# Transposes of two convolution branches and of four head pairs' outputs, moved from TensorE to VectorE blocks and GpSimd's transfers

## What is computed

```python
def reference(x, mem, ...):
    for i in range(DEPTH):                     # DEPTH = 2
        h = _rms_norm(x, pre_norm[i])
        proj = h @ w_in[i]
        tok, q_mem, gate = ...                 # 3*1536 | 512 | 2048 columns
        if i % 2 == 0:
            tok_out = _short_conv_mixer(tok, conv_w[i // 2])      # gate_b * conv3(gate_c * x_in)
        else:
            tok_out = _diff_attention_mixer(tok, positions, ...)  # (softmax1 - lam*softmax2) @ v, normalised per head
        mem_n = _rms_norm(mem, mem_norm[i])
        cross_out = _memory_cross_attention(q_mem, mem_n, w_kv_mem[i])
        y = concatenate([tok_out, cross_out]) * silu(gate) @ w_out[i]
        x = x + _rms_norm(y, post_norm[i])
```

## Time and profile before

| what | value |
|---|---|
| median of three runs | 946.15 us (945.61 to 946.81) |
| the profiled execution, its own time | 946.67 us |
| its span, first to last instruction | 944.9 us |
| granted TensorE clock, mean | 0.998 |
| busy: TensorE, VectorE, ScalarE, GpSimd | 933.8, 636.3, 503.6, 17.2 us |
| share of the chain that ended last: TensorE, VectorE, ScalarE, DMA | 88%, 5%, 2%, 2% |

### The profile page before, as it was taken

One profiled execution on the slowest core, in us unless ns is written; L12 is line 12 of the kernel. 1 busy time (PEld: TensorE's weight loads), 2 busy tenths in 40 slices (PEclk: granted clock), 3 DMA queues, 4 the chain that ended last, 5 costly groups with the idle time before them and its releaser, 6 DMA issues.

```text
span 944.9 us, 12669 instructions
## 1 busy us (share of the span) xinstructions
PE 933.8 (99%) x4752; PEld 789.4 (84%) x4752; DVE 636.3 (67%) x834; ACT 503.6 (53%) x801; POOL 17.2 (2%) x41
## 2 busy tenths in 40 slices
PE   9999999999999999999999999999999999999996
PEld 7888888888888888888888888888888888888885
DVE  5878766754565475555595558557787888888555
ACT  6867553344344443444465555447586576675542
POOL 0000200000000000000000003000000000000000
PEclk9999999999999999999999999999999999999999
DMA  9757585766766666676566658565755746745652
GB/s 330 244 164 230 170 258 177 213 198 214 221 188 191 187 193 220 228 240 231 178 234 192 184 151 255 171 208 154 216 176 159 222 146 187 221 145 173 222 197 89
DMA packets 124894, 188.45 MB, mean 199 GB/s; under 512 B 7277, under 2 KB 66989, under 8 KB 124330
## 3 DMA queue, kind: packets, MB, share of 16 engines
q1 hardware_dynamic: 122138, 178.80, 60.9%
q10 hardware_dynamic: 1680, 6.85, 2.1%
q0 software_dynamic: 1024, 2.10, 0.9%
HBM read 178.82 MB, written 2.10 MB: 191 GB/s over the span
## 4 chain that ended last, share of the span: by engine, by line
PE 88%; DVE 5%; ACT 2%; DMA 2%; issue 2%; SPq 0%; DVEq 0%; POOL 0%; ACTq 0%; POOLq 0%
PE psum L480 19%; PE psum L481 19%; PE psum L482 19%; PE psum L419 17%; PE psum L420 9%; DVE lo_ring L1037 2%; DMA stage_area<-in_mem_dram 1%; PE psum L499 1%; ACT hi_ring L720 1%; DMA layer_area<-layer_area 1%; ACT layer_area L1001 1%; PE psum L661 1%; DMA raw_ring<-in_w_in_dram 0%; ACT stage_area L810 0%; DVE layer_area L1463 0%
## 5 line engine op out<-in xcount | busy, mean ns | idle before, releaser
L1037 DVE TENSOR_TENSOR lo_ring<-raw_ring,hi_ring 128x1024 fp32r<-128x1024 f32 x318 | 385.6, 1222 | 249.0 <-ACT hi_ring L720 248.4
L720 ACT ACTIVATE hi_ring<-raw_ring 128x1024 fp32r<-128x1024 f32 x318 | 335.4, 1061 | 363.0 <-PE psum L482 253.0
L419 PE MATMUL psum<-hT_split,hi_ring 128*128 128x512 f32 x832 | 292.9, 397 | 0.4 <-DVE lo_ring L1037 0.4
L420 PE MATMUL psum<-hT_split,lo_ring 128*128 128x256 f32 x832 | 232.1, 279 | 0.0
L419 PEld LDWEIGHTS psum<-hT_split,hi_ring 128*128 128x128 f32 x832 | 156.1, 188 | 38.8 <-issue 2.0
L480 PE MATMUL psum<-hi_ring,hT_split 128*128 128x512 f32 x480 | 187.0, 390 | 0.4 <-DVE lo_ring L1037 0.4
L481 PE MATMUL psum<-lo_ring,hT_split 128*128 128x512 f32 x480 | 186.8, 389 | 0.0
L482 PE MATMUL psum<-hi_ring,hT_split 128*128 128x512 f32 x480 | 186.8, 389 | 0.0
L420 PEld LDWEIGHTS psum<-hT_split,lo_ring 128*128 128x128 f32 x832 | 156.8, 188 | 0.1
L480 PEld LDWEIGHTS psum<-hi_ring,hT_split 128*128 128x128 f32 x480 | 90.1, 188 | 19.3 <-issue 0.7
L482 PEld LDWEIGHTS psum<-hi_ring,hT_split 128*128 128x128 f32 x480 | 90.1, 188 | 18.9
(11 more groups left out here) (227 smaller groups left out, 754.4 us busy)
## 6 DMA issues: line engine op xcount, KB each, us to landing
raw_ring<-in_w_in_dram SPq DMA_DIRECT2D x224, 512.0 KB, 3.9
raw_ring<-in_w_out_dram SPq DMA_DIRECT2D x64, 512.0 KB, 4.1
raw_ring<-in_w_kv_mem_dram SPq DMA_DIRECT2D x30, 512.0 KB, 4.3
layer_area<-layer_area SPq DMA_DIRECT2D x48, 64.0 KB, 3.7
x_residual<-in_conv_w_dram ACTq DMA_DIRECT2D x3, 768.0 KB, 6.4
stage_area<-in_mem_dram SPq DMA_DIRECT2D x8, 256.0 KB, 6.6
x_residual<-in_x_dram SPq DMA_DIRECT2D x2, 1024.0 KB, 8.6
layer_area<-in_post_norm_dram ACTq DMA_DIRECT2D x2, 1024.0 KB, 6.2
```

What stands on the lines that cost most here:

```text
L419: mm(o, hi[:, k, P * c:P * (c + 1)], X[:, kt, :], start=kt == 0, stop=False)
L420: last = mm(o[:, SEQ:], lo[:, k, P * c:P * (c + 1)], X[:, kt, 0:SEQ], start=False, stop=kt == KT - 1)
L720: run(whi[:, slot, :], raw[:, slot, :], ACT.Copy).then_inc(hi_ready, 1)
L1037: V_.tensor_tensor(wlo[:, slot, :], raw[:, slot, :], whi[:, slot, :].bitcast(f32), SUB)\
```

## The change

Branches 0 and 1 of the convolution, and the outputs of head pairs 0 to 3, are now turned as the memory probabilities were: VectorE turns 32x32 blocks, GpSimd issues 16 transfers, and the result is read from SBUF. Branch 2 and pairs 4 and 5 stay with TensorE. The block turn of layer 0's memory probabilities moves from the last gate group to the first row group of mix 0.

```diff
@@ GpSimd
+        cross_move(0)
+        for j in range(MIXES - 1):
+            pool.wait_ge(b_blocks_turned, 2 * (j + 1))
+            for a, b in QUADRANTS:
+                nc.gpsimd.dma_start(S[32 * b:32 * b + 32, 3072 + 256 * a:3072 + 256 * (a + 1)],
+                                    b_blocks[32 * a:32 * a + 32, 256 * b:256 * (b + 1)]).then_inc(b_blocks_moved, 16)
+        cross_move(1)
+        for p in range(PAIRS - 2):
+            pool.wait_ge(o_blocks_turned, p + 1)
+            for a, b in QUADRANTS:
+                nc.gpsimd.dma_start(oT[32 * b:32 * b + 32, a], o_blocks[32 * a:32 * a + 32, b]).then_inc(o_blocks_moved, 16)
@@ TensorE
-                at = {3: lambda: branch_turn(j - 1)} if j and g == 0 else {4: first_cross_values} if (j, g) == (0, 1) else {}
+                at = {4: first_cross_values} if (j, g) == (0, 1) else {}
...
-            if not first and not second:
-                in_keys[3] = lambda: diff_out_turn(p - 2, p * 8)
@@ ScalarE
+        def branch_rows_high(j):
+            act.wait_ge(b_blocks_moved, 256 * (j + 1))
+            for t in range(TT):
+                last = run(branch_view(j, 0, t), bT[:, t], ACT.Copy)
+            last.then_inc(b_hi, 1)
@@ VectorE
-                     at={2: lambda: cross_blocks(0), 3: lambda: cross_vm_low(0)})
+                     at={3: lambda: cross_vm_low(0)})
...
-            row_group(u, at={5: lambda: branch_low(j - 1)} if j else {})
+            row_group(u, at={1: lambda: branch_blocks(j - 1)} if j else {1: lambda: cross_blocks(0)})
+
+            row_group(u + A_UNITS, at={2: lambda: branch_rows_low(j - 1)} if j else {2: lambda: cross_weights_low(0),
+                                                                                      6: first_cross_branch})
...
+        def out_blocks(p):
+            dve.wait_ge(on_ready, p + 1)
+            V_.transpose(o_blocks.rearrange("p b r g -> p g b r"), o_sb.rearrange("p g (b r) -> p g b r", b=4))\
+              .then_inc(o_blocks_turned, 1)
+
+        def out_moved(st, p, parity):
+            dve.wait_ge(o_blocks_moved, p * 256 + 256)
+            rows_, gate = (v.rearrange("p c (t q) -> p (c t) q", t=TT) for v in (br1, sgate[parity]))
+            V_.scalar_tensor_tensor(rows_, oT.rearrange("p a r g -> p g (a r)"), subg, gate, MULT, MULT).then_inc(o_taken, 1)
+            dve.wait_ge(o_taken, p + 2)
+            split_branch(st, br1, bass.ds(p * 2, 2), in_order=True)
...
+            def norm_and_turn():
+                out_norm(st, p - 2, parity)
+                out_blocks(p - 2)
...
-                in_query[3] = lambda: out_norm(st, p - 2, parity)
-                in_gate[1] = lambda: out_take(st, p - 2, parity)
+                in_query[3] = norm_and_turn
             column_group(G + 2, c + 2, u + 2 * B_UNITS, s, val1, at=in_gate)
+            if not first and not second:
+                out_moved(st, p - 2, parity)
             dve.wait_ge(bank_free, G + 3)
             st.did(silu_twice(p + (MIXES + 3), tanh1, val1, sgate[parity]))
```

More of the change, by code:

```diff
@@ L158, in build @@
     o_sb = l1(5376).rearrange("p (g e) -> p g e", g=4)
+    vm_flat = vm.rearrange("p m e -> p (m e)")
+    o_blocks = vm_flat[:, 0:512].rearrange("p (b r g) -> p b r g", b=4, g=4)
+    oT = vm_flat[:, 512:1024].rearrange("p (a r g) -> p a r g", a=4, g=4)
     o_sq = l1(5888).rearrange("p (g e) -> p g e", g=4)
@@ L175, in build, with branch_view @@
     u_rows, u_before, u_part, b_rows = (rows(S[:, 1024 * i:1024 * (i + 1)]) for i in range(4))
+    b_blocks = S[:, 2048:3072]
+    bT = S[:, 3072:4096].rearrange("p (a c t r) -> p t c a r", a=4, c=4, t=TT)
+    def branch_view(j, first, t):
+        return XC[:, 4 * j:4 * j + 4, first + P * t:first + P * (t + 1)].rearrange("p c (a r) -> p c a r", a=4)
     xg_flat = xgate.rearrange("p h t -> p (h t)")
@@ L243, in build @@
     u_shifted, taps_loaded = sem("u_shifted"), [sem(f"conv_taps_loaded{j}") for j in range(MIXES)]
+    b_blocks_turned, b_blocks_moved = sem("branch_blocks_turned"), sem("branch_blocks_moved")
+    o_blocks_turned, o_blocks_moved = sem("o_blocks_turned"), sem("o_blocks_moved")
     b_ready, b_turned, b_hi = sem("branch_rows_ready"), sem("branch_rows_turned"), sem("branch_hi")
@@ L385, in _, with cross_move @@
                                 pattern=[[-1, P]], channel_multiplier=1).then_inc(const_ready, 1)
-        for l in range(DEPTH):
+        def cross_move(l):
             pool.wait_ge(xblocks_turned, 4 * (l + 1))
@@ L633, in _, with diff_values @@
                 cross_values(1)
-        def diff_values(p):
+        def diff_values(p, first=False):
             pe.wait_ge(wt_ready, p * 16 + 16)
+            if not first:
+                pe.wait_ge(o_blocks_turned, p)
             for h in range(2):
@@ L643, in diff_values, with diff_out_turn @@
             last.then_inc(pv_done, 1)
-        def diff_out_turn(p, exps=None):
+        def diff_out_turn(p):
             pe.wait_ge(on_ready, p + 1)
-            if exps is not None:
-                pe.wait_ge(exp_done, exps)
+            pe.wait_ge(exp_done, PAIRS * 8)
             for g in range(4):
@@ L669, in pair @@
                 in_query[1] = lambda: diff_scores(p - 1, second)
-                in_gate[1] = lambda: diff_values(p - 1)
-            if not first and not second:
-                in_keys[3] = lambda: diff_out_turn(p - 2, p * 8)
+                in_gate[1] = lambda: diff_values(p - 1, second)
             column_group(G, u, s, XA, at=in_query)
@@ L688, in last_values @@
         def last_values():
-            diff_out_turn(PAIRS - 2, PAIRS * 8)
-            diff_values(PAIRS - 1)
+            diff_out_turn(PAIRS - 2)
+            diff_values(PAIRS - 1, True)
         for g in range(4):
@@ L915, in _ @@
         tanh_of(G_XG0 + 1, val0, xin)
+        def branch_rows_high(j):
[3 more added lines that the diff above has]
+            last.then_inc(b_hi, 1)
         def branch_high(j):
-            act.wait_ge(b_turned, j + 1)
+            act.wait_ge(b_turned, 1)
             run(XC[:, 4 * j:4 * j + 4, 0:SEQ], ps[:, 4:6, :].rearrange("p b (h t) -> p (b h) t", h=2), ACT.Copy)\
@@ L929, in _ @@
                 if g == 0:
-                    row_group(G, u, G % 2, x_rows, at={4: lambda: branch_high(j - 1)} if j else {})
+                    row_group(G, u, G % 2, x_rows)
                 else:
-                    ahead(u, A_UNITS, {2: last_taps} if (j, g) == (1, 1) else {0: lambda: cross_take(0)} if (j, g) == (0, 1) else {})
+                    ahead(u, A_UNITS, {} if g != 1 else {0: lambda: branch_rows_high(j - 1), 2: last_taps} if j == 1
+                          else {0: lambda: branch_rows_high(j - 1)} if j else {0: lambda: cross_take(0)})
                 if g == 3:
@@ L1286, in first_cross_branch, with branch_blocks, branch_rows_low @@
             st.did(V_.memset(u_before[0:1, :, :], 0.0))
+        def branch_blocks(j):
+            dve.wait_ge(b_ready, j + 1)
+            for t in range(TT):
+                V_.transpose(b_blocks.rearrange("p (b c t r) -> p t c b r", b=4, c=4, t=TT)[:, t],
+                             b_rows[:, t, :].rearrange("p (c b r) -> p c b r", c=4, b=4)).then_inc(b_blocks_turned, 1)
+        def branch_rows_low(j):
+            dve.wait_ge(b_hi, j + 1)
+            for t in range(TT):
+                hi_v, lo_v = branch_view(j, 0, t), branch_view(j, SEQ, t)
+                last = V_.tensor_tensor(lo_v, bT[:, t], hi_v.bitcast(f32), SUB)
+            last.then_inc(branch_ready, 1)
         def branch_low(j):
@@ L1332, in _ @@
             if j:
-                dve.wait_ge(b_turned, j)
+                dve.wait_ge(branch_ready, j + 1)
             dve.wait_ge(tanh_done, 3 + j)
```

3 lines of the change are left out of this document (1 added, 2 removed).

## The result

| | before | after |
|---|---|---|
| median of four runs each | 946.25 us (945.61 to 946.81) | 957.12 us (955.42 to 958.47) |
| ratio, 95% interval | | 1.0116, 1.0103 to 1.0128 |
| the profiled execution: own time, span | 946.67, 944.9 us | 955.42, 953.6 us |
| granted clock, mean, profiled execution | 0.998 | 0.996 (0.993 in the three others) |

The account below looks back on a forecast made before the run. TensorE, busy 99% of the span, was taken to bound the kernel. -1.76 + 0.72 + 6.3 + 1.75 = +7.0 on the profiled 946.67 gave 953.7, or 953.2 us against the median; range 950.3 to 958.

Parts of the forecast that it names:

- rival (a): The main case: TensorE waits at the scores and low part as reckoned, own range 951 to 957 us; 72%.
- steps that double: Upper side of the main case: four-float steps double both VectorE operations, +0.5 us at each of eight places, +3.9.
- Transposes of the branches, -1.76: Branches 0 and 1 lose eight TensorE transposes each, 0.88 us saved per branch, 1.76 for two.
- the same four units: Layer 0: ScalarE's ring of four units, 2.7 us each, hides a 1 or 2 us miss by the later memory weights.
- Layer 0 hidden: Layer-0 block turns and transfers end by 219.7, ScalarE wants them at 223.7: four us to spare, cost nothing.
- Pair 2, +0.72: Only the block turn is new in pair 2; TensorE goes on after its low part at 696.91 instead of 696.19.
- The wait at the scores, +1.75: TensorE's scores wait for `o_taken`, now raised behind the `combine`: +1.75 us in pairs 3 to 5 and behind the loop.
- The chain, +2.1 a pair: Pairs 3 to 5: VectorE's chain from `combine` to the late low part delays TensorE 2.1 us each, scores' wait contained.
- Steps in all: Four-float steps in the block turn and `out_moved`'s first operation: +0.2 us each; without them 1.6 come off.
- (b): More waiting: `combine` 1.21 us after the scores at three other ends, 3.2 more, 956.9; or transfers late for `out_moved`; 12%.
- Rival (d): Faster: moved outputs don't hold TensorE, only the 32 removed transposes count, -3.6 us, 942.6; 7%.
- The rule that was weighed ahead of the prediction: SBUF lines of 16 bytes: fp32 may step over four elements free, giving 952.1 profiled; but a line needs two hits.

Follow-up runs that it names:

- second group: The same changed kernel, unedited, run again at the end of the experiments: 955.56 us, ratio 1.0094 to the kernel before.
- the branches alone: Against the changed kernel: only the branches and the memory weights of the change, pair outputs turned by TensorE as before; 944.76 us, ratio 0.9985.
- the weights early: The kernel with only the branches changed, the memory weights' block turn back at its old place in the last gate group: 944.5 us, ratio 0.9987.
- the kernel without steps: Changed kernel with block buffer and `oT` laid out so VectorE writes and reads runs, transfers in pieces of 128 bytes: 951.38 us, ratio 1.0056.
- first try: Changed kernel: pair p-1 normalised and block-turned one gate group earlier, `out_moved` in the keys group, pair 4 moved too, no 16-byte steps, no scores' wait: 956.76 us.
- last schedule: Against the first try: `out_moved` at index 2 of the keys group, keys' rotation at index 2 of the gate group, memory weights early; 944.26 us.
- scores free: Changed kernel without TensorE's wait for `o_taken` at the scores, everything still computed: 957.97 us, ratio 1.0126.
- blocks behind: Changed kernel with the outputs' block turn moved from the query group's last place to index 1 of the keys group: 954.93 us, ratio 1.0088.

## Why the prediction came out as it did

The prediction was 953.2 us with a range of 950.3 to 958.0, "slower" at 89%; measured 957.12, and 955.56 in the second group. The side and the mechanism were right, the size was 3.9 us too small (2.4 by the second group). The measured time lies just above rival (a)'s own range of 951 to 957; the stated range holds it since it left room for steps that double. Step by step:

- **Transposes of the branches, -1.76.** About right: -1.5 by the medians with the branches alone, and in it is what the memory weights cost. Those I had put at nothing, "a miss of 1 or 2 us lies under the same four units". The units did cover ScalarE. What I had not looked at is TensorE's own use of the weights right behind: its first matmul with them started 0.23 us after the one ahead of it, and now starts 141.83 - 141.34 = 0.49 after. With the weights early the medians still say -1.5, so 0.26 more or less is within their scatter.
- **Layer 0 hidden.** Right. GpSimd's transfers for the branches took 496 ns each and 4.0 us at most to land, and no unit of mixes 0 to 2 waits for a high or low part. ScalarE's high parts start at 223.1 (I had 223.7).
- **Pair 2, +0.72.** With the first wait at the scores I had 0.72 + 1.75 = 2.47 up to pair 3's scores, and 2.89 is measured. The two steps' extra price, 0.21 and 0.19, accounts for it: 2.87.
- **The wait at the scores, +1.75.** 1.94, 1.78, 1.88, 1.95 measured. The step failed in one term only: "I take +0.2, what three floats show". The operation took 1134 ns, 0.39 more than without steps.
- **The chain, +2.1 a pair, the scores' wait contained in it.** Right in kind, and shown: with the scores' wait taken away the same time stands at the low part. In size it is 2.40 in pair 3, with +0.38 and +0.41 for the two steps where I had 0.2 each: 2.1 + 0.39 = 2.5. Pair 4 shows +1.38 in one execution and 40.23 - 37.84 = +2.39 in the other, of which some is clock. It had lost 0.41 before already, and I did not take that off. Against the kernel with the branches only, the pairs without a low clock cost 39.58 - 37.05 = 2.53, 39.22 - 36.78 = 2.44 and, in the second execution, 39.43 - 37.00 = 2.43: the predicted chain with the steps' measured price, in all three pairs.
- **Steps in all.** 0.21 in pair 2, 3 x 0.39, and 0.18 behind the loop: 1.6 us more than predicted. Without any cost of steps the prediction gives 953.2 - 1.6 = 951.6, and the kernel without steps measured 951.38. That it meets so closely is in part luck. In the two traces the last matmul of the kernel without steps comes 941.19 - 936.79 = 4.4 us after that of before, where the sum without steps has 5.4; nearly all of the difference is pair 4 (+0.64 instead of 1.7), because before was slow there. The terms were right but for the steps' price, and the clock was missing.
- **The clock.** Missing in the prediction. 957.12 less 953.2 less 1.6 leaves 2.3 us. The profiled execution had one low stretch and a mean of 0.996, the second one two and 0.994; the first try above had three and 0.993. The three other runs of the first group show 0.993, so probably three each. At 0.8 to 1.6 us apiece that makes the 2.3 or more. It is an estimate, since only two of the eight executions have a trace. The run with a mean of 0.998 took 953.85, 0.95 under the 953.2 + 1.6 = 954.8 of the sum with the steps' true price; so some of the clock's cost is offset by a sum that was a little too large elsewhere, as far as one run can tell.

Of the rivals, (b) named nearly the right time, 956.9, and the wrong causes. Its first was that `combine` comes 1.21 us after the scores at the other ends of pairs too; it starts at 714.02, 753.60, 792.82 and 833.09, within 0.11 us of when TensorE was ready for the scores. Its second was a late transfer: none was late. It had "an issue takes over 0.8 us" as its point, and the issues stayed at 496 to 498 ns:

```profile
L414 POOL DMA_DIRECT2D vm<-vm x64: 496/496/498, 694.8 to 821.0; - x64
...
DMA to landing us min/median/max: 1.6/3.5/5.3
```

Rival (d), the mere gain of 3.6 us, is not even reached by the last schedule, which has no wait at the scores left (-1.8).

The rule that was weighed ahead of the prediction, the Trainium skill's "SBUF — State Buffer", Door 1, has two halves. That fp32 may step over four elements for free is not what these traces show: +58% on the write of the block turn (1122 against 712 ns), +53% on the read (1134 against 742). The other half, that a line wants two hits, points the right way. The row of three floats (+23%) lay between.

What stays open: what decides behind which of several waits of 1.8 to 2.6 us the clock falls. And the full reason why the kernel with the branches only and the one with all outputs moved end at the same time: half of the loss in each pair is the low part that comes 0.31 us late, the other half is not placed, and no run took either away.

## What to carry to other kernels

When a transpose goes from the bound engine to an engine that hands it work, follow the new work along that engine's order to the next thing the bound engine asks for: here 0.45 us of transposes a pair were paid for with 2.4 to 2.5 us of a chain that had no air, while the same move in the convolution, with 4 us of air, was a gain. Removing the wait in front of the chain gave nothing here; taking time out of the chain gave 0.8 us a pair, and putting its operations elsewhere helped only where they made nothing else late. And where VectorE is on the path, let the transfers carry the awkward layout: 50 ns more per issue on an idle engine took 0.8 us a pair off VectorE and kept TensorE's clock up.

## What the runs showed of the hardware that was not expected

- Steps of four floats (16 bytes) cost VectorE about half as much again, on a write (1122 against 712 ns for 128x512) as on one of two read operands (1134 against 742). Steps of three cost 847 against 690.
- The granted clock fell to 0.50 for about 3.4 us behind single waits of TensorE of 1.8 us and more, in an otherwise full stream, and behind none of those of up to 1.7. It fell behind 1 of 4 such waits (after), 2 of 4 (after, again), 2 of 3 (scores free), 2 of 4 (blocks behind) and 3 of 4 (first try). Such a wait may cost nearly twice its length (behind the loop a wait of 1.85 us, and 1.6 more at the low clock). The clock has the two levels of which the Trainium skill speaks ("TensorE: Matmul & The Clock Gate", Part 1), 0.50 and 1.00 in all the windows above but that in which it changes. The same program lost it in pair 5 in one execution, and in pair 4 and behind the loop in the next.
- A transfer of 32 partitions in pieces of 128 bytes took GpSimd 548 ns to issue and landed after 1.7 to 6.5 us; in pieces of 512 bytes it was 496 ns and 1.6 to 5.3 us.
